# A long depthwise convolution beside a state-space scan: one of eight channel groups computed by ScalarE and GpSimd

## The chip, the cores and the metric

The kernel runs on one core of a Trainium2 chip, in one launch. The metric is the time of the device in microseconds. The kernel before takes 2796.59 us, the median of three runs (2795.34 to 2796.99).

## The reference

The reference computes, for 512 tokens of width 1024, one block of attention with its MLP (`first_block`) and then two layers of a second block (`second_block`), all in fp32. The change lies in the mixer of the second block's first layer, the "even" mixer:

```python
def even_mixer(x, w_in, conv_w, conv_b, conv_ln_g, conv_ln_b, ssm_conv_w, ...):
    proj = x @ w_in
    conv_val, conv_gate, z, xbc, dt = jnp.split(proj, [c0, c1, c2, c3], axis=-1)
    u = conv_val * jax.nn.sigmoid(conv_gate)
    u = causal_depthwise_conv(u, conv_w, conv_b)        # 31 taps, 1024 channels
    u = jax.nn.silu(layer_norm(u, conv_ln_g, conv_ln_b))
    xbc = jax.nn.silu(causal_depthwise_conv(xbc, ssm_conv_w, ssm_conv_b))   # 4 taps
    ...
    y = ssd_chunked(xs * dt, dt * a, bm, cm)            # scan over 4 chunks of 128 tokens
    y = (y + xs * d_skip) * jax.nn.silu(z)
    y = rms_norm(y by group of 512)
    return jnp.concatenate([u, y], axis=-1) @ w_out
```

The layer goes on with a cross attention over 256 memory tokens and an MLP. The products that make the memory's keys and values do not depend on the mixer.

## The kernel before, in words

**Products.** Channels lie on the 128 partitions, tokens in the free dimension. Every fp32 product is made of three products of rounded fp32 ("fp32r"): high activation by high weight, low activation by high weight, high activation by low weight (L923, L925, L927). A *unit* is one group of 128 output channels for 512 tokens: 24 matmuls of 128x128 by 128x512. For each of the eight tiles of the depth the three follow each other in that order, so the third matmul of a unit is the first that reads the low weight. ScalarE rounds each weight tile (L1539, `round_ahead` L1528), VectorE (L2323) or GpSimd (L3412, `lower_ahead`) subtracts the rounded tile from the original and so makes the low part. Three tiles of high weights and five raw tiles are held; each engine rounds or lowers up to two units ahead, at the place where its own program calls `run_steps` or `round_ahead`. In the gate and value part of the even mixer GpSimd makes the low parts. DMA queues of SyncE load the weights.

**Order.** No scheduler runs on the chip: each engine has its own instruction list, written out by a Python function for it, and the engines meet at semaphores. A wait in a list holds everything that stands behind it on that engine. The lists follow one plan (`plans`, from L296). For the even mixer it is:
- "ev lead" and "ev gv": 8 gate units (`evg`) and 8 value units (`evv`), three of them in the lead, and between them `dt`. Counted from 0, the 14 steps of "ev gv" are evv1, dt, evg2, evg3, evv2, evv3, evg4, evg5, evv4, evv5, evg6, evg7, evv6, evv7. VectorE makes the product of value and sigmoid after each value unit (L2494).
- "ev xbc": 10 units in the order 0, 1, 2, 3, 8, 10, 4, 5, 6, 7, then "ev xbc end": 9 and 11. Each is copied from PSUM by ScalarE (L1526), convolved with 4 taps by VectorE (L2508), and made into silu by `xbc_half` (ScalarE, L1721, with L1725 and L1729) and `xbc_end` (VectorE, L2456), which come one unit later, behind the next unit's short convolution.
- 16 scan steps (4 chunks by 4 quarters of the heads). For each, ScalarE makes `E1` (L2012) and four exponentials, VectorE the masked decay (`scan_mask` L2968, `scan_decay` L2980), GpSimd two products (L3551, L3562), TensorE the products. Every second step carries one `z` unit. Before them, at step 6 of "ev gv", ScalarE makes the exponential `dte` (L1999), for which VectorE has computed the exponent (`step_widths` L2903, L2954, L2957).
- The gated rms norm (squares by L3036, sums by TensorE at L1008), the first half of the output product (`yout`), with the memory's value and key units (`mv`, `mk`; 256 tokens) between its units.
- "conv wait": three memory units. Then the sums of the convolution's layer norm over all channels (L1350 to L1356), the eight `("conv norm", k)` parts with one or two memory units each, and the rest of the output product.

**The long convolution.** The 1024 channels are 8 groups of 128. ScalarE makes tap 0 of a group into a PSUM bank (`conv_first` L1954) and VectorE adds taps 1 to 30 there, one instruction each, `bank = input shifted by t times tap weight + bank` (`long_tap` L2443, L2450). Two banks hold two groups at a time: even groups in bank 3, odd ones in bank 7 (`conv_bank`, L707). The taps of two groups are interleaved, since each tap reads the sum that the last one of its group wrote; an interleaved tap takes some 0.66 us, one that directly follows another of its group some 0.79. After tap 30 ScalarE copies the group out with its bias and makes its square (`conv_out` L1964, L1968, L1974), GpSimd adds both to the running sums (`conv_inputs` L3528), and `conv_first(m + 2)` takes the bank again.

All 240 taps of VectorE have slots (L736 to L753): 6 in the lead, 8 behind each of the 14 steps of "ev gv", 3 behind each of the first 8 xbc units, 3 in each scan step, 2 to 5 in the items of "y out", and the rest, 7, in "conv wait". The ends of the groups follow from it:

| group | 0 | 1 | 2 | 3 | 4 | 5 | 6 | 7 |
|---|---|---|---|---|---|---|---|---|
| ends in slot | gv 5 | gv 6 | gv 13 | xbc unit 0 | scan 10 | scan 12 | y out 13 | conv wait |

`conv_out(slot)` stands in ScalarE's list behind the unit of that slot, and so ahead of the rounding of the weights for the next unit that has not been rounded yet.

**Places for the rest.** `zT` holds the gated z, 8 groups; it is not written before the scan. `sq_rings["conv"]` holds the squares on their way to GpSimd.

The slots of the taps in the kernel before, lines 740 to 744:

```python
        tap_slots = {("gv", "lead"): 6} | {("gv", i): 8 for i in range(14)} | {("xbc", m): 3 for m in XBC_ORDER[:8]}
        tap_slots |= {("scan", st): 3 for st in STEPS}
        out_items = plans["y lead"] + plans["y out"]
        tap_slots |= {("y out", i): 0 if isinstance(u, Step) else 3 if u.name != "yout" else 2 if i < 3 else 5
                      for i, u in enumerate(out_items)}
```

## Time and profile before

| | |
|---|---|
| median of three runs | 2796.59 us (2795.34 to 2796.99) |
| the profiled execution | 2796.68 us, of which the span of the instructions is 2794.9 |
| TensorE's mean granted clock | 0.972 |
| TensorE matmul busy | 2659.7 us, 95% |
| VectorE busy | 1477.1 us, 53% |
| ScalarE busy | 1123.1 us, 40% |
| GpSimd busy | 406.5 us, 15% |
| the 240 taps of VectorE (L2450) | 167.9 us |
| the 91 low parts of GpSimd (L3412) | 195.5 us |

The profile is of one execution. All times in rows are from the start of its span. The profiled execution took 1.8 us more than its span: what lies before the first and behind the last instruction. Engines are named PE (TensorE's matmuls), PEld (its weight loads, which lie beside matmuls), DVE (VectorE), ACT (ScalarE) and POOL (GpSimd). The granted clock is a share of full speed: 1.0 is 2.4 GHz and a half is 1.2 GHz. The part of the even mixer that the change touches runs from about 1000 us to about 1435 us: gate and value part to 1110, xbc to 1190, scan to 1272, its end and the gated norm to 1301, the first half of the output product with the memory's units to 1361, the convolution's norm to 1435.

In a row of a timeline the brackets say for how long the engine had stood idle before the instruction, and which instruction's end let it go on.

### The profile page before, as it was taken

The page shows a single profiled execution, that of the slowest core. Times are in us where ns is not written, and L with a number is a line of the kernel's source. Part 1 is how long each engine was busy: PE and PEld are TensorE (multiplying, and loading weights), DVE is VectorE, ACT ScalarE, POOL GpSimd, SP SyncE. Part 2 cuts the span into 40 slices and gives each one's busy share as a digit, 9 for nine tenths or more (in the row PEclk, how much of TensorE's full clock was granted, in tenths as well). Part 3 has the DMA queues.
Part 4 walks back from the last instruction along what each step waited for, and adds up shares of the span by engine and source line. Part 5 has one row for each costly group of instructions (what it writes and reads, how often), then busy time and mean ns, then how long its engine had stood idle before and what let it go on. Part 6 is the DMA issues. An engine that isn't in the chain of part 4 may idle for free.

```text
span 2794.9 us, 33638 instructions
## 1 busy us (share of the span) xinstructions
PE 2659.7 (95%) x13661; PEld 2192.6 (78%) x13661; DVE 1477.1 (53%) x2551; ACT 1123.1 (40%) x1845; POOL 406.5 (15%) x295
## 2 busy tenths in 40 slices
PE   6998799999999999998999999999999999999998
PEld 6775567778888987786886778889788886888887
DVE  3366866345333279798874643333734743642334
ACT  2455344235332243645554443322642543542323
POOL 0032123110000024443110111000000100110000
PEclk6999899999999999999999999999999999999999
DMA  8343223442333333212431233333221341233331
GB/s 222 98 109 82 76 69 94 118 112 83 98 92 97 91 85 85 81 38 68 129 90 53 68 91 91 98 92 90 76 83 38 102 125 45 84 91 98 92 97 61
DMA packets 483306, 251.31 MB, mean 90 GB/s; under 512 B 15582, under 2 KB 480050, under 8 KB 483151
## 3 DMA queue, kind: packets, MB, share of 16 engines
q1 hardware_dynamic: 480596, 242.56, 30.8%
q0 software_dynamic: 1840, 5.59, 0.6%
q8 instruction: 107, 1.75, 0.3%
q10 hardware_dynamic: 715, 1.01, 0.1%
q14 instruction: 48, 0.39, 0.0%
HBM read 247.00 MB, written 2.13 MB: 89 GB/s over the span
## 4 chain that ended last, share of the span: by engine, by line
PE 79%; DVE 13%; ACT 6%; issue 1%; POOL 0%; DMA 0%; SPq 0%; POOLq 0%; DVEq 0%; ACTq 0%
PE ps L927 19%; PE ps L923 19%; PE ps L925 19%; PE ps L859 2%; PE ps L855 2%; PE ps L857 2%; PE ps L949 2%; DVE ps L2450 2%; PE ps L883 1%; DVE w_r L2323 1%; PE ps L1395 1%; PE ps L1078 1%; PE ps L873 1%; PE ps L875 1%; PE ps L1093 1%
## 5 line engine op out<-in xcount | busy, mean ns | idle before, releaser
L923 PE MATMUL ps<-XH,wh 128*128 128x512 f32 (+2 forms) x1896 | 769.2, 406 | 11.0 <-ACT arena_f L1729 3.7
L927 PE MATMUL ps<-XH,w_r 128*128 128x512 f32 (+2 forms) x1896 | 753.6, 397 | 5.8 <-DVE w_r L2323 4.0
L925 PE MATMUL ps<-XL,wh 128*128 128x512 f32 x1776 | 709.0, 399 | 3.0 <-DVE XL L2834 2.8
L2323 DVE TENSOR_TENSOR w_r<-w_f,wh 128x1024 fp32r<-128x1024 f32 (+1 forms) x316 | 378.7, 1200 | 566.5 <-ACT wh L1539 566.4
L1539 ACT ACTIVATE wh<-w_f 128x1024 fp32r<-128x1024 f32 (+2 forms) x407 | 411.0, 1012 | 390.6 <-PE ps L927 209.9
L923 PEld LDWEIGHTS ps<-XH,wh 128*128 128x128 f32 (+2 forms) x1896 | 359.3, 190 | 120.1 <-issue 19.7
L927 PEld LDWEIGHTS ps<-XH,w_r 128*128 128x128 f32 (+2 forms) x1896 | 357.6, 189 | 94.3 <-DVE w_r L2323 6.6
L925 PEld LDWEIGHTS ps<-XL,wh 128*128 128x128 f32 x1776 | 335.5, 189 | 86.0 <-issue 4.4
L925 PE MATMUL ps<-arena_r,wh 128*128 128x512 f32 (+1 forms) x936 | 343.1, 367 | 0.0
L923 PE MATMUL ps<-arena_r,wh 128*128 128x512 f32 (+1 forms) x726 | 265.1, 365 | 1.4 <-ACT wh L1539 1.4
L927 PE MATMUL ps<-arena_r,w_r 128*128 128x512 f32 (+1 forms) x726 | 259.9, 358 | 6.2 <-DVE w_r L2323 6.2
L3412 POOL TENSOR_TENSOR w_r<-w_f,wh 128x1024 fp32r<-128x1024 f32 (+4 forms) x91 | 195.5, 2150 | 421.2 <-ACT wh L1539 421.1
L925 PEld LDWEIGHTS ps<-arena_r,wh 128*128 128x128 f32 x936 | 178.1, 190 | 30.7 <-issue 1.9
L857 PE MATMUL ps<-arena_r,wh 128*128 128x256 f32 x672 | 188.9, 281 | 0.0
L2450 DVE SCALAR_TENSOR_TENSOR ps<-arena_f,vec,ps 128x512 f32<-128x512 f32 x240 | 167.9, 750 | 6.9 <-ACT ps L1526 5.9
L1688 ACT ACTIVATE arena_f<-ps 128x512 f32<-128x512 f32 x96 | 57.1, 595 | 266.6 <-PE ps L927 252.5
L927 PEld LDWEIGHTS ps<-arena_r,w_r 128*128 128x128 f32 x726 | 138.6, 191 | 28.2 <-DVE w_r L2323 7.2
L923 PEld LDWEIGHTS ps<-arena_r,wh 128*128 128x128 f32 x726 | 138.7, 191 | 27.7 <-issue 5.4
L1526 ACT ACTIVATE arena_f<-ps 128x512 f32<-128x512 f32 (+6 forms) x198 | 89.5, 468 | 171.1 <-PE ps L927 120.5
L3459 POOL TENSOR_TENSOR arena_f<-arena_f 128x512 f32<-128x512 f32 x48 | 55.0, 1145 | 536.8 <-ACT arena_f L1688 536.8
L857 PEld LDWEIGHTS ps<-arena_r,wh 128*128 128x128 f32 x672 | 126.9, 189 | 0.4
L855 PE MATMUL ps<-arena_r,wh 128*128 128x256 f32 x420 | 118.6, 282 | 0.0
(383 smaller groups left out, 3816.2 us busy)
## 6 DMA issues: line engine op xcount, KB each, us to landing
w_f<-in_mlp_w SPq DMA_DIRECT2D x126, 512.0 KB, 4.1
w_f<-in_w_ff SPq DMA_DIRECT2D x63, 512.0 KB, 4.0
w_f<-in_w_in SPq DMA_DIRECT2D x49, 512.0 KB, 3.8
w_f<-in_ada_w SPq DMA_DIRECT2D x35, 512.0 KB, 4.0
w_f<-in_even_w_in SPq DMA_DIRECT2D x35, 512.0 KB, 3.8
w_f<-in_odd_w_in SPq DMA_DIRECT2D x23, 512.0 KB, 3.8
w_f<-in_even_w_out SPq DMA_DIRECT2D x16, 512.0 KB, 4.1
w_f<-in_xa_w_v SPq DMA_DIRECT2D x16, 512.0 KB, 4.1
```

What stands on the lines that cost most here:

```text
L855: e.matmul(b, hi[:, k, :], xh[:, hs], start=u.first and k == 0, stop=False)
L857: e.matmul(b, hi[:, k, :], xl[:, hs], start=False, stop=False)
L859: last = e.matmul(b, lo[:, k, :], xh[:, hs], start=False, stop=u.final and k == u.kc - 1)
L923: e.matmul(b, hi[:, k, :], xh, start=u.first and k == 0, stop=False)
L925: e.matmul(b, hi[:, k, :], xl, start=False, stop=False)
L927: last = e.matmul(b, lo[:, k, :], xh, start=False, stop=u.final and k == u.kc - 1)
L1526: return e.activation(o, i, ACT.Copy, scale=scale).then_inc(act.sem, act.up(*mark))
L1539: e.activation(high_flat(u), flat(u, 0), ACT.Copy).then_inc(act.sem, act.up("high", u.n))
L1688: e.activation(ffn_h[:, m, :], b, ACT.Relu).then_inc(act.sem, act.up("ff relu", st, m))
L2323: e.tensor_tensor(flat(u, 1), flat(u, 0), high_flat(u).bitcast(F32), ALU.subtract).then_inc(dve.sem, dve.up("low", u.n))
L2450: e.scalar_tensor_tensor(out=o, in0=val[:, m, t:t + S], scalar=conv_tap(t, m), in1=o, op0=ALU.mult, op1=ALU.add).then_inc(dve.sem, dve.up( ...
L3412: e.tensor_tensor(flat(u, 1), flat(u, 0), high_flat(u).bitcast(F32), ALU.subtract).then_inc(pool.sem, pool.up("low", u.n))
```

## The change

- **One group off VectorE.** `POOL_GROUP = 2`. Its sum stands in `zT[:, 7]` in SBUF. ScalarE makes tap 0 there, and each further tap as a scaled copy into one of four tiles (`scaled(t)` is `zT[:, 3 + t % 4]`); GpSimd adds it to the sum. Three taps stand behind each of the steps 5 to 13 of "ev gv" and one behind each of the first three xbc units, after the engine's `run_steps` of that step. ScalarE's copy of tap t waits for GpSimd's add of tap t - 4, and each add for the one before. The group is copied out and squared behind the eighth xbc unit (5 is its channel group).
- **210 taps on VectorE in other slots**: 6 in the lead, 7 behind each step of "ev gv", 3 behind each of the ten xbc units of "ev xbc", 6 in a new slot "xbc end" between the short convolutions of units 9 and 11, 2 in each scan step, 1, 2 or 4 in the items of "y out", and 7 in "conv wait". Groups 0, 3, 5, 7 and 1, 4, 6 follow each other in the two banks. The groups end as follows:

| group | 0 | 1 | 2 | 3 | 4 | 5 | 6 | 7 |
|---|---|---|---|---|---|---|---|---|
| ends in slot | gv 6 | gv 7 | xbc unit 5 | xbc unit 2 | xbc unit 10 | y out 0 | y out 6 | conv wait |

- **Weights rounded first.** Where a group ends, ScalarE calls `round_ahead` for the next unit before it waits for the group's last tap (`conv_out(..., before=...)`).
- **The end of xbc.** The silu parts of the last three units (7, 9, 11) no longer stand behind the next unit's short convolution: `xbc_half(7)` stands behind ScalarE's first exponential of the scan, and `xbc_end(7)` behind VectorE's `scan_mask(0)`; those of 9 and 11 stand directly behind their own units.
- **The sums of the convolution's norm** come in TensorE's list behind one memory unit, not three. The norm's parts 0 and 1 have two memory units each, not 2 and 1, so that no unit is added or dropped.
- GpSimd adds the groups to the running sums in the order in which they end (`conv_input`). No product and no tap is left out.

The diff, cut to its core:

```diff
-    plans["conv wait"] = [next(kv) for _ in range(3)]
+    plans["conv wait"] = [next(kv) for _ in range(2)]
     for k in range(KC):
-        plans["conv norm", k] = [next(kv) for _ in range(1 if k else 2)]
+        plans["conv norm", k] = [next(kv) for _ in range(2 if k < 2 else 1)]
...
-        conv_bank = [banks[3], banks[7]]
+
+        conv_at = [banks[3 if j % 2 == 0 else 7] for j in range(KC)]
+        conv_at[POOL_GROUP:] = [zT[:, KC - 1, :]] + conv_at[POOL_GROUP:-1]
+
+        def scaled(t):
+
+            return zT[:, 3 + t % 4, :]
...
-        tap_slots |= {("scan", st): 3 for st in STEPS}
+
+        groups = [m for m in range(KC) if m != POOL_GROUP]
+        taps = [(groups[0], t) for t in range(1, CONV_W)]
+        for j in range(1, len(groups)):
+            ahead = 6 if j % 2 else 28
+            at = (j - 1) * (CONV_W - 1) + ahead
+            taps[at:] = [v for t in range(1, CONV_W)
+                         for v in ([(groups[j - 1], t + ahead)] if t + ahead < CONV_W else []) + [(groups[j], t)]]
+        tap_slots = {("gv", "lead"): 6} | {("gv", i): 7 for i in range(14)} | {("xbc", m): 3 for m in XBC_ORDER[:XBC_FIRST]}
+        tap_slots |= {("xbc end",): 6}
+        tap_slots |= {("scan", st): 2 for st in STEPS}
         out_items = plans["y lead"] + plans["y out"]
-        tap_slots |= {("y out", i): 0 if isinstance(u, Step) else 3 if u.name != "yout" else 2 if i < 3 else 5
+        tap_slots |= {("y out", i): 0 if isinstance(u, Step) else 2 if i == 4 or u.name != "yout" else 1 if i < 3 else 4
                       for i, u in enumerate(out_items)}
-        tap_slots["conv wait",] = (CONV_W - 1) * KC - sum(tap_slots.values())
...
+        pool_taps = {("gv", i): 3 for i in range(5, 14)} | {("xbc", m): 1 for m in XBC_ORDER[:3]}
...
-            run("conv wait")
+            run_units(plans["conv wait"][:1])
...
             sq_rings["conv"].free(pe, "conv", KC - 1)
+            run_units(plans["conv wait"][1:])
             for k in range(KC):
...
-                    if m:
+                    if 0 < XBC_ORDER.index(m) < XBC_FIRST:
                         xbc_half(XBC_ORDER[XBC_ORDER.index(m) - 1])
...
+                if m in groups[:2]:
+                    w.wait_ge(*(lin, att4)[groups.index(m)].held("conv"))
+                elif m != POOL_GROUP:
+                    w.wait_ge(act, "sq", "conv", groups[groups.index(m) - 2])
...
+            def own_taps(*slot):
+
+                for t in [next(tap_of) for _ in range(pool_taps.get(slot, 0))]:
+                    if t > 4:
+                        w.wait_ge(pool, "conv", POOL_GROUP, t - 4)
+                    copy(scaled(t), val[:, POOL_GROUP, t:t + S], "tap", t, scale=conv_tap(t, POOL_GROUP))
...
+                e.activation(conv[:, m, :], conv_at[m][:, :], ACT.Identity, bias=column("even_conv_b_2", m)).then_inc(
...
+                if m in groups[:-2]:
+                    conv_first(groups[groups.index(m) + 2])
+
+            def conv_out(*slot, before=None):
...
                 for m in conv_ends[slot]:
-                    w.wait_ge(dve, "conv", m)
...
-                    if m + 2 < KC:
-                        conv_first(m + 2)
+                    if before:
+                        round_ahead(before.n)
+                    conv_end(m, dve)
...
 
             conv_first(0)
+            nexts = dict(zip(plans["ev gv"] + plans["ev xbc"], plans["ev gv"][1:] + plans["ev xbc"] + plans["ev xbc end"]))
             for i, u in enumerate(plans["ev gv"]):
                 run_steps([u])
-                if i == 0:
-                    conv_first(1)
+                if u.name == "evv" and u.m in (groups[1], POOL_GROUP):
+                    conv_first(u.m)
                 if i == 3:
                     flush()
                     log1p_exp_minus(dt_, sc1, sc2, sc3, "dt")
                 if i == 6:
                     w.wait_ge(dve, "dte")
                     e.activation(dte, dte, ACT.Exp).then_inc(act.sem, act.up("dte"))
-                conv_out("gv", i)
+                own_taps("gv", i)
+                conv_out("gv", i, before=nexts[u])
...
                 e.activation(E1, bb, ACT.Exp).then_inc(act.sem, act.up("e1", st))
+                if st == 0:
+                    xbc_half(XBC_ORDER[XBC_FIRST - 1])
...
             for u in plans["ev xbc"]:
                 run_steps([u])
-                if ("xbc", u.m) in conv_ends:
-                    conv_out("xbc", u.m)
+                own_taps("xbc", u.m)
+                conv_out("xbc", u.m, before=nexts[u])
+                if u.m == XBC_ORDER[7]:
+                    conv_end(POOL_GROUP, pool)
             scan_groups(0, 0)
             scan_decay(0)
-            run("ev xbc end")
-            xbc_half(XBC_ORDER[-1])
+
+            zs = {st: plans["scan", st | 1][0] for st in STEPS}
+            for u in plans["ev xbc end"]:
+                run_steps([u])
+                xbc_half(u.m)
+                if u.m == XBC_ORDER[XBC_FIRST]:
+                    conv_out("xbc end", before=plans["ev xbc end"][1])
...
-                conv_out("scan", st)
+                conv_out("scan", st, before=zs.get(st))
...
-                    conv_out("y out", n)
-            run_steps(plans["conv wait"][:2])
-            conv_out("conv wait")
-            run_steps(plans["conv wait"][2:])
+                    conv_out("y out", n, before=plans["conv wait"][0] if i == len(out_items) - 1 else None)
+            conv_out("conv wait", before=plans["conv wait"][0])
+            run("conv wait")
...
             scan_mask(0)
+            xbc_end(XBC_ORDER[XBC_FIRST - 1])
             scan_decay(0)
-            run("ev xbc end")
+            run_steps(plans["ev xbc end"][:1])
+            conv_taps("xbc end")
+            xbc_end(XBC_ORDER[XBC_FIRST])
+            run_steps(plans["ev xbc end"][1:])
             xbc_end(XBC_ORDER[-1])
...
+            def own_taps(*slot):
+
+                o, m = conv_at[POOL_GROUP], POOL_GROUP
+                for t in [next(tap_of) for _ in range(pool_taps.get(slot, 0))]:
+                    w.wait_ge(act, "tap", t)
+                    if t > 1:
+                        w.wait_ge(pool, "conv", m, t - 1)
+                    e.tensor_tensor(o, o, scaled(t), ALU.add).then_inc(pool.sem, pool.up("conv", m, t))
+                    if t == CONV_W - 1:
+                        pool.marks["conv", m] = pool.count
...
+                own_taps("xbc", u.m)
+                conv_inputs("xbc", u.m)
+                if u.m == XBC_ORDER[7]:
+                    conv_input(POOL_GROUP)
...
-            run("ev xbc end")
+            run_steps(plans["ev xbc end"][:1])
+            conv_inputs("xbc end")
+            run_steps(plans["ev xbc end"][1:])
```

## Rows read from the trace of the kernel before

**Rows 1.** The page: engine busy time, and the chain that ended last
```profile
PE 2659.7 (95%) x13661; PEld 2192.6 (78%) x13661; DVE 1477.1 (53%) x2551; ACT 1123.1 (40%) x1845; POOL 406.5 (15%) x295
...
PE 79%; DVE 13%; ACT 6%; issue 1%; POOL 0%; DMA 0%; SPq 0%; POOLq 0%; DVEq 0%; ACTq 0%
```

**Rows 2.** Busy time by stretch: PE, PEld, DVE, ACT, POOL, granted clock, DMA share, GB/s
```profile
1015.00:1110.00 95.00, 90.38 (x394) 70.47 (x393) 88.55 (x137) 30.16 (x42) 37.79 (x19) 0.96 0.32 89
...
1190.00:1272.00 82.00, 81.84 (x514) 71.21 (x512) 75.47 (x138) 38.54 (x95) 40.39 (x31) 0.98 0.14 39
...
1272.00:1301.00 29.00, 19.50 (x78) 14.23 (x79) 27.33 (x42) 20.34 (x30) 6.70 (x4) 0.82 0.22 73
```

**Rows 3.** Timeline, TensorE alone: start us, us, what [idle before <-releaser]
```profile
1069.09 0.79 PE L927 MATMUL ps<-XH,w_r 128*128 128x512 f32 x1 [1.71 <-POOL w_r L3412]
...
1082.26 0.39 PE L923 MATMUL ps<-XH,wh 128*128 128x512 f32 x1
...
1116.15 0.40 PE L927 MATMUL ps<-XH,w_r 128*128 128x512 f32 x1
...
1171.65 0.50 PE L923 MATMUL ps<-XH,wh 128*128 128x512 f32 x1 [2.78 <-ACT arena_f L1729]
...
1281.61 0.46 PE L1253 MATMUL ps<-arena_f 128*128 128x128 f32 x2 [4.20 <-DVE arena_f L2980]
...
1296.19 2.08 PE L1008 MATMUL ps<-stat,ones 128*128 128x512 f32 x2 [2.17 <-DVE stat L3036]
...
1366.11 0.58 PE L927 MATMUL ps<-arena_r,w_r 128*128 128x256 f32 x1 [3.33 <-DVE w_r L2323]
...
1405.83 0.50 PE L927 MATMUL ps<-XH,w_r 128*128 128x512 f32 x1 [1.10 <-DVE w_r L2323]
```

**Rows 4.** Timeline, ScalarE alone
```profile
1063.57 0.69 ACT L1968 ACTIVATE arena_f<-ps,vec 128x512 f32<-128x512 f32 x1 [16.01 <-DVE ps L2450]
...
1065.50 1.04 ACT L1539 ACTIVATE wh<-w_f 128x1024 fp32r<-128x1024 f32 x1
...
1070.29 0.26 ACT L1999 ACTIVATE arena_f<-arena_f 128x64 f32<-128x64 f32 x1 [1.84 <-DVE arena_f L2957]
...
1267.24 0.69 ACT L1968 ACTIVATE arena_f<-ps,vec 128x512 f32<-128x512 f32 x1 [2.28 <-DVE ps L2450]
...
1377.26 1.28 ACT L1651 ACT_TABLE_LOAD   x1
```

**Rows 5.** Timeline, VectorE alone
```profile
1019.50 4.71 DVE L2450 SCALAR_TENSOR_TENSOR ps<-arena_f,vec,ps 128x512 f32<-128x512 f32 x6 [0.76 <-ACT ps L1526]
...
1052.38 0.68 DVE L2494 SCALAR_TENSOR_TENSOR arena_f<-gates,ps 128x512 f32<-128x512 f32 x1
...
1123.51 1.23 DVE L2456 SCALAR_TENSOR_TENSOR arena_f<-arena_f 128x512 f32<-128x512 f32 x1
...
1178.84 2.34 DVE L2508 SCALAR_TENSOR_TENSOR ps<-arena_f,vec,ps 128x512 f32<-128x512 f32 x3 [5.45 <-ACT ps L1526]
...
1269.78 0.69 DVE L2968 TENSOR_TENSOR arena_f<-ps,const 128x512 f32<-128x512 f32 x1 [2.58 <-ACT arena_f L2012]
...
1357.46 7.48 DVE L2450 SCALAR_TENSOR_TENSOR ps<-arena_f,vec,ps 128x512 f32<-128x512 f32 x10
...
1379.22 0.75 DVE L3133 SCALAR_TENSOR_TENSOR arena_f<-arena_f,vec,stat 128x512 f32<-128x512 f32 x1 [0.94 <-ACT stat L1651]
```

**Rows 6.** GpSimd: timeline, and one tile's instructions (duration ns min/median/max)
```profile
1073.55 7.12 POOL L3412 TENSOR_TENSOR w_r<-w_f,wh 128x1024 fp32r<-128x1024 f32 x3
...
L3459 POOL TENSOR_TENSOR arena_f<-arena_f x48: 1040/1041/1671, 660.3 to 2592.9; 128x512 f32<-128x512 f32 x48
...
L3551 POOL TENSOR_TENSOR arena_f<-arena_f x16: 1262/1276/1369, 1163.9 to 1278.2; 128x512 f32<-128x512 f32 x16
...
2072.57 0.63 POOL L3626 TENSOR_SCALAR_AFFINE_SELECT arena_f<-arena_f 128x512 f32<-128x512 f32 x1 [107.78 <-ACT arena_f L1526]
...
2073.28 0.42 POOL L3629 TENSOR_SCALAR_AFFINE_SELECT arena_f<-arena_f 128x256 f32<-128x256 f32 x1
```

More of the change, by code:

```diff
@@ L73 @@
 XBC_FIRST = 10
+POOL_GROUP = 2
 def t5_bucket(n):
@@ L731, in program @@
         split_to = splits_of()
-        taps = [(0, t) for t in range(1, CONV_W)]
-        for m in range(1, KC):
-            ahead = 6 if m % 2 else 28
-            at = (m - 1) * (CONV_W - 1) + ahead
-            taps[at:] = [v for t in range(1, CONV_W) for v in ([(m - 1, t + ahead)] if t + ahead < CONV_W else []) + [(m, t)]]
-        tap_slots = {("gv", "lead"): 6} | {("gv", i): 8 for i in range(14)} | {("xbc", m): 3 for m in XBC_ORDER[:8]}
-        tap_slots |= {("scan", st): 3 for st in STEPS}
+        groups = [m for m in range(KC) if m != POOL_GROUP]
[8 more added lines that the diff above has]
+        tap_slots |= {("scan", st): 2 for st in STEPS}
         out_items = plans["y lead"] + plans["y out"]
-        tap_slots |= {("y out", i): 0 if isinstance(u, Step) else 3 if u.name != "yout" else 2 if i < 3 else 5
+        tap_slots |= {("y out", i): 0 if isinstance(u, Step) else 2 if i == 4 or u.name != "yout" else 1 if i < 3 else 4
                       for i, u in enumerate(out_items)}
-        tap_slots["conv wait",] = (CONV_W - 1) * KC - sum(tap_slots.values())
+        tap_slots["conv wait",] = (CONV_W - 1) * len(groups) - sum(tap_slots.values())
         slot_taps, conv_ends, taps_done = {}, {}, 0
@@ L752, in program @@
             taps_done += n
-        assert sorted(v for ts in slot_taps.values() for v in ts) == [(m, t) for m in range(KC) for t in range(1, CONV_W)]
+        assert sorted(v for ts in slot_taps.values() for v in ts) == [(m, t) for m in groups for t in range(1, CONV_W)]
+        pool_taps = {("gv", i): 3 for i in range(5, 14)} | {("xbc", m): 1 for m in XBC_ORDER[:3]}
+        assert sum(pool_taps.values()) == CONV_W - 1
         def chunk_of(u, k):
@@ L1954, in conv_first @@
             def conv_first(m):
-                if m < 2:
-                    w.wait_ge(*(lin, att4)[m].held("conv"))
-                else:
-                    w.wait_ge(act, "sq", "conv", m - 2)
+                if m in groups[:2]:
+                    w.wait_ge(*(lin, att4)[groups.index(m)].held("conv"))
+                elif m != POOL_GROUP:
+                    w.wait_ge(act, "sq", "conv", groups[groups.index(m) - 2])
                 w.wait_ge(dve, "val", m)
                 w.wait_ge(dve, "half taps")
-                copy(conv_bank[m % 2][:, :], val[:, m, 0:S], "first", m, scale=conv_tap(0, m))
@@ L1964, in conv_out @@
-            def conv_out(*slot):
-                for m in conv_ends[slot]:
-                    w.wait_ge(dve, "conv", m)
-                    e.activation(conv[:, m, :], conv_bank[m % 2][:, :], ACT.Identity, bias=column("even_conv_b_2", m)).then_inc(
-                        act.sem, act.up("conv out", m))
-                    s = conv_q
-                    if m:
-                        s, freed = sq_rings["conv"].take("conv", m)
-                        w.wait_ge(*freed)
-                    e.activation(s, conv_bank[m % 2][:, :], ACT.Square, bias=column("even_conv_b_2", m)).then_inc(
-                        act.sem, act.up("sq", "conv", m))
-                    if m + 2 < KC:
-                        conv_first(m + 2)
+                copy(conv_at[m][:, :], val[:, m, 0:S], "first", m, scale=conv_tap(0, m))
@@ new lines, in scalar_program, with conv_end @@
+            tap_of = iter(range(1, CONV_W))
+            def own_taps(*slot):
[3 more added lines that the diff above has]
+                    copy(scaled(t), val[:, POOL_GROUP, t:t + S], "tap", t, scale=conv_tap(t, POOL_GROUP))
+            def conv_end(m, progress):
+                w.wait_ge(progress, "conv", m)
+                e.activation(conv[:, m, :], conv_at[m][:, :], ACT.Identity, bias=column("even_conv_b_2", m)).then_inc(
+                    act.sem, act.up("conv out", m))
+                s = conv_q
+                if m:
+                    s, freed = sq_rings["conv"].take("conv", m)
+                    w.wait_ge(*freed)
+                e.activation(s, conv_at[m][:, :], ACT.Square, bias=column("even_conv_b_2", m)).then_inc(
+                    act.sem, act.up("sq", "conv", m))
+                if m in groups[:-2]:
+                    conv_first(groups[groups.index(m) + 2])
@@ L2443, in long_tap @@
             def long_tap(m, t):
-                o = conv_bank[m % 2][:, :]
+                o = conv_at[m][:, :]
                 if t == 1:
@@ L2511, in evacuate @@
                     raw_ring.free(dve, m)
-                    if m:
+                    if 0 < XBC_ORDER.index(m) < XBC_FIRST:
                         xbc_end(XBC_ORDER[XBC_ORDER.index(m) - 1])
```

28 lines of the change are left out of this document (17 added, 11 removed).

## The prediction, before the result was known

> **What bounds the kernel now.** I read the page first: TensorE is busy for 95% of the span and is most of the chain that ended last [rows 1]. Only its idle time and its half-speed time can be won. The busy time by stage comes next [rows 2]: the even mixer is where VectorE is nearly as busy as TensorE. TensorE's waits there, and the single matmuls after each wait [rows 3], give four places. (a) 1063.6 to 1069.1: idle 5.1 us in the gate and value part. (b) 1168.7 to 1171.65: 2.9 us, a bank that xbc unit 9 holds. (c) 1277 to 1296: the end of the scan, 4.4 us before the last output step and more before the products and the sums of the gated norm. (d) 1361 to 1366.1: low weights behind the last taps. In the scan proper (1190:1272) TensorE is busy for all 82 us though VectorE is too: taps taken out of there win nothing by themselves, they only let VectorE reach the scan's end less late.
>
> **The sum** is made against the profiled execution, 2796.7 us (span 2794.9), 0.1 above the median of the three runs, 2796.6. Signs: plus is slower. "Unit" is one 24-matmul product, 5.57 us.
>
> **1. Place (a): the new rounding point.** Now ScalarE waits for group 0's last tap until 1063.57, only then rounds (1065.50), GpSimd lowers, and TensorE gets its low weights at 1069.09 [rows 3, 4]. The change rounds ahead of the sums, and VectorE has 7 taps a slot, not 8. But at step 6 ScalarE has a second wait ahead of all this: dte (row L1999 at 1070.29), which VectorE makes behind slot 6's taps [rows 4, 5]. The new time of dte: evv2's product at 1052.4 - 0.66 = 1051.7 (one tap fewer in the dt chain); two times (0.6 + 7 x 0.66) = 10.4 to 1062.2; nacs and 7 taps, 4.9, to 1067.1; dte read by ScalarE at 1067.3. Behind it in ScalarE's queue stand the exponential 0.2, three scaled taps 1.8 and the rounding 1.1: to 1070.4. GpSimd must add taps 4 to 6 first (from 1068.1, 3.9) and then lower (2.4): 1074.5. The unit that stalled now runs 1063.6 to 1069.2, and the next one, at its third matmul at 1069.7, waits for that low part: 4.8 us, against 5.1. The stall moves one unit on; the half-speed stretch that follows it (mean granted clock 0.96 over these 95 us [rows 2]) moves with it. Term: **0** (that unit ended at 1082.26, it would end at 1082.2). The three ScalarE operations per step cost nothing more here: ScalarE is busy 30 of 95 us [rows 2].
>
> **2. GpSimd as the bound.** From gv step 5 GpSimd has, per unit, one lowering, 2.38 us, and three adds into one accumulator. No row shows this add. Its nearest row is L3551, 128x512 in the same arena with two different inputs: 1.28 [rows 6]. Each add waits for the one before; a waiting pair there starts 0.07 after its predecessor's end (L3626 0.63, L3629 0.71 later), an independent one 0.04 before it. So a step costs 2.38 + 1.35 + 1.35 + 1.24 = 6.3 us where TensorE needs 5.57. From tap 4 at 1068.1 up to the low part of the third xbc unit stand in GpSimd's queue: 8 lowerings 19.0, 24 adds 31.5, and the two sum adds of group 1, 2.5: 53.0, to 1121.1. That unit's third matmul ran at 1116.15 [rows 3]. Term: **+5.0**, seen as some 0.7 us of idle in each of seven units. The lower bound is L3459's 1.04 (both inputs the same tile): 5.5 a step, no bound, term 0. The upper bound is its longest, 1.67: 24 x 0.39 more, term +14.4. I take 1.28, by the row with two inputs. ScalarE's wait for a free one of four slots (tap t for add t - 4) holds nobody: three adds stand ready whenever it waits.
>
> **3. xbc and its end.** Place (b) goes: unit 9's half is made right after the first exponential. But units 6 and 7 now have three taps between their short convolution (2.0 us later), and six taps (4.0) stand between the short convolutions of units 9 and 11. Unit 11's short convolution ended at 1181.2 [rows 5]; on the old clock it would now end at 1163.8 + 2.0, xbc_end, inputs and mask 1.9, exponentials and rounding 2.3, copies 1.3, short convolution 2.3, taps 4.0, xbc_end 0.6, short convolution 2.3: 1180.5. TensorE waits for it in the first scan steps instead of at (b). Three group ends move into xbc, each 2 us of ScalarE, within a bank's slack of 3 us. Term: **-0.5** (bounds 0 and -2.9).
>
> **4. The end of the scan.** 16 taps leave it, 10.6 us of VectorE, and both group ends. ScalarE's 2.3 us wait for a tap at 1267.24, which made the mask late (1269.78) [rows 4, 5], is gone. Seg 14 comes from TensorE at 1266.2 as now; exponential, mask, exponentials and product of step 14 end at 1269.9, group inputs (4.6 beside a lowering) at 1274.9, z 1275.5, mask 15 1276.2, exponentials 1277.5, product 1278.4, where TensorE now starts at 1281.61 [rows 3]: 3.2 earlier. After that one tap less and no lag: rstd at 1285.3, first high part at 1286.8 (was 1291.4), the g1 sums at 1291.4 where they ran at 1296.19. Term: **-4.8** (bounds: 0 if another wait holds the chain; -8.0 if the half-speed stretches behind 0.82 [rows 2] go too).
>
> **5. Output part.** TensorE has no gap from 1300 to 1361, so 12 taps fewer win nothing before the last ones. Group 7's last 13 taps now stand alone, in series at 0.79 (the ten at 1357.46 took 7.48, seven of them in series [rows 5]), with one lowering: 1353.0 + 10.3 + 1.1 = 1364.4, against 1364.8. The sums no longer stand behind two value products, so TensorE idles from 1359 to 1365.1 and they end at 1367.1 at half speed, not 1374.9. But ScalarE now evacuates a value product that runs behind them before its tables and the rstd: the product ends at 1371.8, two evacuations 0.8, two table loads of 1.28 [rows 4], logarithm and exponential 1.4, so 1376.5, against 1379.2 for the first norm [rows 5]. VectorE then carries ten lowerings, not nine (+1.1), to the one that releases the output products at 1405.83 [rows 3]. Term: -2.7 + 1.1 = **-1.6** (bounds 0 and -3.4, the latter with TensorE never waiting after the sums).
>
> **Total**: 0 + 5.0 - 0.5 - 4.8 - 1.6 = -1.9. Predicted 2794.8 us. A change of 0.2%, 5.6 us, is about what a measurement of this kernel can tell from none.
>
> **Rivals.**
> **A, cheap adds.** The add costs 1.04 like L3459, the median of its 48 rows. Then term 2 is 0 and the time 2794.8 - 5.0 = 2789.8. Against it: L3551, with two different inputs, never went below 1.26 [rows 6]. The Trainium skill ("GPSIMD Engine Reference", 3.1 Elementwise) gives about 2.6 cycles an element for a two-input add; at that page's 1.2 GHz an estimate of 1.1 us for 512, which would take 4 us from term 2 and put the time at 2790.7. L3551's row is 0.17 above that figure. Chance 0.18.
> **B, the stall at (a) really goes.** If dte is ready early, GpSimd's queue of 53.0 starts at 1062.8 and ends at 1115.8, before the third xbc unit needs it at 1116.15: terms 1 and 2 together are -0.3, not +5.0, and the time 2794.8 - 5.3 = 2789.5. For it: the rounding is what the old chain waits for. Against it: dte's wait stands in the code and in the trace. Chance 0.15.
> **C, the tail gives nothing back.** Another wait takes the scan's end (the squares, the table loads of 1.28): term 4 is 0, 2799.6. Chance 0.1.
> **D, slower: adds and taps hold each other.** L3459 has rows of 1.67, and a VectorE product with both inputs in SBUF goes from 0.68 to 1.23 beside GpSimd [rows 5, 6]. If each add cost 1.67, term 2 is +14.4 and the time 2804. It decides from an add of 1.6 us. Against it: a tap has one operand in PSUM, and 6 of them took 4.71 beside a lowering, the usual 0.66 each [rows 5]. Chance 0.12.
> **The forecast case**: 0.45, its own range 2790.5 to 2798.5.
> That the change does not do what it says would be seen in the counts below; the diff leaves no room for it.
>
> **The numbers.** The range takes A, B, C and the forecast with their bounds: 2788.5 to 2801. Faster by over 0.2% (under 2791.0): most of A and B and a tail of the forecast, 0.31. Slower by over 0.2% (over 2802.2): D and a little of C, 0.13. Between: 0.56.
>
> **What would show it.** Step 1: no idle at the unit that starts at 1063.6, some 5 us at the next one, ended by GpSimd's low part, and ScalarE waiting for dte at about 1067. Step 2: GpSimd busy over 90% from 1068 to 1121, adds 1.28 long at 1.35, TensorE waiting for L3412's low part seven times. Step 3: no wait for L1729 before unit 11. Step 4: the last scan output 3 us less behind its predecessor. Step 5: 30 fewer taps on VectorE (210), TensorE idle before the conv sums. I am wrong if TensorE's waits for GpSimd come to less than 3 us or more than 9, or if a fresh wait of over 2 us stands in the scan or the output part.

## The result, and the profile after

The changed kernel takes 2802.24 us, the median of 20 runs (2799.45 to 2803.39), against 2795.66 for the kernel before (2794.39 to 2798.18) in the same 20 rounds: a ratio of 1.0022, 95% interval 1.0015 to 1.0029. It is 6.6 us slower. 2794.8 was forecast, and the range ended at 2801. The profiled execution took 2802.54, its span is 2800.8, 5.9 above the span before.

The experiments below are medians of 5 to 11 runs, in three sets of rounds: e1 to e4, with the kernel before at 2796.60 in the same rounds; e5 to e8, with it at 2796.25; e9 and e10, with it at 2796.06. The figure behind each median is the ratio to the kernel before of its own rounds, with its 95% interval. In the last set two runs at a mean clock of 0.647 and 0.554 (3727 us for e9, 4331 us for the kernel before) stand apart from all others, and the ratios leave them out.

The page of the kernel after, first its busy times, then the chain that ended last, then the group of TensorE's third matmuls (busy, mean, and how long it stood idle before them):

```profile
PE 2661.7 (95%) x13661; PEld 2190.9 (78%) x13661; DVE 1456.9 (52%) x2521; ACT 1142.8 (41%) x1875; POOL 447.7 (16%) x325
...
PE 78%; DVE 11%; ACT 6%; issue 3%; POOL 2%; DMA 0%; SPq 0%; POOLq 0%; DVEq 0%; ACTq 0%
...
L942 PE MATMUL ps<-XH,w_r 128*128 128x512 f32 (+2 forms) x1896 | 752.9, 397 | 12.9 <-POOL w_r L3457 8.9
```

Against [rows 1] VectorE has 30 instructions fewer, ScalarE and GpSimd 30 more each, and GpSimd now has 2% of the chain, where it had none. The last row holds most of the loss: TensorE waits 8.9 us for low parts that GpSimd makes (L3412 before is L3457 now; L927 is L942). With the wait of 3.62 us at 1318.96 below, which stands in another row of the page, its waits for GpSimd's low parts are ten and come to 12.5 us; before they were two and 1.9.

Busy time by stretch, columns as in [rows 2]:

```profile
1015.00:1110.00 95.00, 87.52 (x382) 67.24 (x381) 76.81 (x122) 45.01 (x65) 62.38 (x39) 0.98 0.32 89
...
1190.00:1272.00 82.00, 80.09 (x508) 70.40 (x508) 70.79 (x134) 35.55 (x91) 36.52 (x30) 0.96 0.14 39
1272.00:1301.00 29.00, 22.96 (x100) 17.59 (x100) 26.44 (x40) 21.77 (x34) 7.25 (x5) 0.82 0.24 73
1301.00:1361.00 60.00, 56.38 (x297) 47.81 (x296) 35.77 (x51) 20.86 (x31) 23.72 (x12) 0.97 0.33 96
```

VectorE fell from 88.6 to 76.8 us in the gate and value part, GpSimd rose from 37.8 to 62.4, and TensorE fell from 90.4 to 87.5: the work left VectorE, for which TensorE had waited only around place (a) of the prediction, and went to the engine for which it then waited in every unit. TensorE, eight of its waits in the order of time:

```profile
1073.41 0.50 PE L942 MATMUL ps<-XH,w_r 128*128 128x512 f32 x1 [3.54 <-POOL w_r L3457]
...
1082.13 0.50 PE L942 MATMUL ps<-XH,w_r 128*128 128x512 f32 x1 [1.34 <-POOL w_r L3457]
...
1121.03 0.50 PE L942 MATMUL ps<-XH,w_r 128*128 128x512 f32 x1 [0.65 <-POOL w_r L3457]
...
1188.27 0.30 PE L1291 MATMUL ps<-const,arena_f 128*128 128x128 f32 x1 [2.93 <-DVE arena_f L2497]
...
1282.43 0.35 PE L1268 MATMUL ps<-arena_f 128*128 128x128 f32 x1 [1.90 <-DVE arena_f L3021]
...
1318.96 0.50 PE L942 MATMUL ps<-arena_r,w_r 128*128 128x512 f32 x1 [3.62 <-POOL w_r L3457]
...
1370.62 1.22 PE L1369 MATMUL ps<-arena_f,ones 128*128 128x512 f32 x1 [4.93 <-ACT arena_f L1992]
...
1411.39 0.50 PE L942 MATMUL ps<-XH,w_r 128*128 128x512 f32 x1 [1.09 <-DVE w_r L2364]
```

The row at 1318.96 has no counterpart in [rows 3]: before, TensorE was busy from 1300 to 1361 without a gap.

TensorE's 13,661 matmuls stand in the same order in all these kernels, but for a few around the convolution's sums. So the start of the same-numbered matmul in two traces can be compared, and the difference at 1003 us, ahead of the change, taken off (it is 0.3 for the kernel after, and between -1.6 and 1.7 for the experiments). The columns are times of the kernel before, the entries microseconds later than before (negative is earlier). Each line is one execution; those of e6 and e10 are the slowest of their runs, 3.5 and 3.2 us above the median:

```
                  1119    1189    1271    1299    1328    1357    1473    2391    2791
after             4.71    4.65    3.88   -0.10    5.29    5.29    5.29    5.45    5.57
e1 sums later     4.69    4.62    3.91   -0.08   -0.05   -0.05   -0.76   -3.75   -4.11
e2 two adds      -3.53   -2.52   -3.07   -7.30   -3.29   -3.29   -2.54   -4.01   -3.81
e3 both          -3.55   -2.55   -3.07   -7.28   -7.08   -7.08   -6.10   -7.77   -7.61
e4 round only     1.76    3.29    5.11    3.75    3.41    3.41    3.42    3.51    3.45
e5 four adds     11.28   11.22   10.63    6.47    6.65    6.65    6.01    2.79    3.02
e6 dte later     -7.06   -6.06   -6.53  -10.81  -10.53  -10.53   -9.56  -11.11  -10.88
e7 tail only      0.01    0.02    0.00    0.00   -0.01   -0.01   -0.41   -0.19   -0.36
e8 tail back     -3.53   -2.51   -3.05   -7.26   -7.06   -7.06   -7.31   -7.19   -7.61
e9 no end taps   -7.05   -7.82   -9.11  -13.09  -13.35  -13.35  -19.43  -20.87  -21.17
e10 scan three   -7.05   -6.05   -3.87   -4.44   -3.93   -3.93   -6.08   -7.77   -7.62
```

The first line is the whole story of the change: 4.7 lost up to the third xbc unit, nothing in xbc, 4.75 won back in the scan (0.8 in its first steps, 4.0 at its end), and 5.4 lost between 1309 and 1328: 3.8 by the wait and 1.6 by the half speed that follows it (1320.4 to 1323.8). GpSimd there, and the same engine in the gate part:

```profile
1088.53 4.19 POOL L3603 TENSOR_TENSOR arena_f<-arena_f 128x512 f32<-128x512 f32 x3
1092.67 2.40 POOL L3457 TENSOR_TENSOR w_r<-w_f,wh 128x1024 fp32r<-128x1024 f32 x1
1095.03 4.17 POOL L3603 TENSOR_TENSOR arena_f<-arena_f 128x512 f32<-128x512 f32 x3
...
1314.31 1.08 POOL L3580 TENSOR_TENSOR stat<-stat,arena_f 128x512 f32<-128x512 f32 x1 [26.54 <-ACT arena_f L1992]
1315.36 1.26 POOL L3585 TENSOR_TENSOR arena_f<-arena_f,sq 128x512 f32<-128x512 f32 x1
1316.58 7.00 POOL L3457 TENSOR_TENSOR w_r<-w_f,wh 128x1024 fp32r<-128x1024 f32 x3
```

At 1314 GpSimd has been idle for 26.5 us. ScalarE had rounded a weight tile by about 1312.5, but GpSimd could not lower it: the two adds of group 5 into the running sums stand ahead in its list, and they wait for ScalarE's copy of the group. The low part was ready at 1318.9; before, GpSimd began it at 1312.5. The reason is a difference between two lists. `conv_out` and `conv_inputs` both follow the slots, but ScalarE calls those of the items 0, 1 and 2 of "y out" together at item 2, behind its roundings, and GpSimd calls each at its own item. The low parts of the next units come behind item 0 (in e1 below two of them stand ahead of the moved sums, and the third behind). Before, no group ended in items 0 to 2. Now group 5 ends in item 0.

### The profile page after: what moved, and what is told of

It reads as the page before. It is cut to its first block, busy times and chain, and to the rows that moved or that the text cites. A ratio compares the mean times of both kernels' runs of the same rounds, so it can differ in the third digit from the quotient of the medians.

```text
span 2800.8 us, 33696 instructions
## 1 busy us (share of the span) xinstructions
PE 2661.7 (95%) x13661; PEld 2190.9 (78%) x13661; DVE 1456.9 (52%) x2521; ACT 1142.8 (41%) x1875; POOL 447.7 (16%) x325
## 4 chain that ended last, share of the span: by engine, by line
PE 78%; DVE 11%; ACT 6%; issue 3%; POOL 2%; DMA 0%; SPq 0%; POOLq 0%; DVEq 0%; ACTq 0%
PE ps L942 19%; PE ps L938 19%; PE ps L940 19%; PE ps L874 2%; PE ps L870 2%; PE ps L872 2%; PE ps L964 2%; PE ps L898 1%; DVE ps L2491 1%; PE ps L1411 1%; PE ps L888 1%; PE ps L1093 1%; PE ps L890 1%; DVE w_r L2364 1%; POOL arena_f L3603 1%
## 5 line engine op out<-in xcount | busy, mean ns | idle before, releaser
L942 PE MATMUL ps<-XH,w_r 128*128 128x512 f32 (+2 forms) x1896 | 752.9, 397 | 12.9 <-POOL w_r L3457 8.9
L942 PEld LDWEIGHTS ps<-XH,w_r 128*128 128x128 f32 (+2 forms) x1896 | 356.7, 188 | 104.0 <-POOL w_r L3457 12.8
L942 PE MATMUL ps<-arena_r,w_r 128*128 128x512 f32 (+1 forms) x726 | 259.4, 357 | 6.1 <-POOL w_r L3457 3.6
L3457 POOL TENSOR_TENSOR w_r<-w_f,wh 128x1024 fp32r<-128x1024 f32 (+4 forms) x91 | 194.6, 2141 | 351.3 <-ACT wh L1555 351.3
L942 PEld LDWEIGHTS ps<-arena_r,w_r 128*128 128x128 f32 x726 | 137.9, 190 | 28.3 <-POOL w_r L3457 4.0
L2491 DVE SCALAR_TENSOR_TENSOR ps<-arena_f,vec,ps 128x512 f32<-128x512 f32 x210 | 148.7, 750 | 14.5 <-ACT ps L1542 12.9
```

Source lines behind the costliest of these rows:

```text
L942: last = e.matmul(b, lo[:, k, :], xh, start=False, stop=u.final and k == u.kc - 1)
L2491: e.scalar_tensor_tensor(out=o, in0=val[:, m, t:t + S], scalar=conv_tap(t, m), in1=o, op0=ALU.mult, op1=ALU.add).then_inc(dve.sem, dve.up( ...
L3457: e.tensor_tensor(flat(u, 1), flat(u, 0), high_flat(u).bitcast(F32), ALU.subtract).then_inc(pool.sem, pool.up("low", u.n))
```

## The experiments

**e1, the sums behind the low parts.** GpSimd's list is brought in line with ScalarE's.

```diff
                     lower_ahead(u.n)
-                conv_inputs("y out", i)
+                if i >= 2:
+                    for n in (0, 1, 2) if i == 2 else (i,):
+                        conv_inputs("y out", n)
```

> Edit of the changed kernel: GpSimd adds group 5 to the running sums behind its three low parts of item 2 of "y out", not ahead of them. Theory Q (GpSimd's queue): TensorE's idle time of 3.8 us at 1315 and the slow clock behind it go, the time falls by 5 us from 2802.2 to about 2797. Rival V (the wait moves): the low part is late for another reason, or the late sums delay the convolution's sums; then the stall stays within 1 us or comes back before 1375, and the time is 2801 to 2803.

Measured: 2793.17 us, 0.9991 of before (0.9982 to 1.0000). By the table the stall is gone, 5.3 us between 1299 and 1328. GpSimd's timeline in e1:

```profile
1313.25 4.77 POOL L3457 TENSOR_TENSOR w_r<-w_f,wh 128x1024 fp32r<-128x1024 f32 x2 [24.94 <-ACT wh L1555]
1317.99 1.08 POOL L3580 TENSOR_TENSOR stat<-stat,arena_f 128x512 f32<-128x512 f32 x1
```

Theory Q holds for the place and the size. The median fell by 9.1, not 5: the other 3 to 4 us stand behind 1473, in a part that no edit touches (below, on the clock). Against the kernel before the interval reaches 1.0000: e1 is hardly to be told from it.

**e2, two adds a step.**

```diff
-        pool_taps = {("gv", i): 3 for i in range(5, 14)} | {("xbc", m): 1 for m in XBC_ORDER[:3]}
+        pool_taps = {("gv", i): 2 for i in range(5, 14)} | {("xbc", m): 2 if j < 4 else 1 for j, m in enumerate(XBC_ORDER[:8])}
```

> Edit of the changed kernel: the same 30 taps of group 2, two (not three) behind each step 5 to 13 of "ev gv", the other 12 over the first eight xbc units. Theory Q: GpSimd needs 2.38 + 2 x 1.38 = 5.1 us a step, under TensorE's 5.57; the seven gaps of 0.8 us from 1080 to 1121 go, the time falls by 5 to 2797. Rival S (adds and taps share something: each add slows VectorE or TensorE's operands wherever it stands): the number of adds is the same, so the loss stays, 2801 to 2803, and VectorE's or TensorE's instructions are longer than before in the xbc units.

Measured: 2792.60, 0.9984 (0.9975 to 0.9992). The column 1119 falls from 4.71 to -3.53, by 8.2 where 5 were expected: the repeated gaps are gone, and the first stall is shorter too (idle 2.14 instead of 3.54, since two adds and not three stand ahead of that low part, and no half-speed stretch at 1075). The number of adds is the same, so rival S falls. Group 5's stall is still there, 3.61 us at 1311.54; no half speed follows it here, and it costs 3.8 us (columns 1299 and 1328), where it cost 5.4 in the kernel after.

**e3, both.** e1's and e2's edits together.

> Both edits of the changed kernel together (sums behind the low parts, two adds a step). Theory Q: both losses go, 10 us, to about 2792, 3.5 us under the kernel before (2795.7), which is what the scan's end and the convolution's norm give back. Rival V: time won in the gate part is lost again at the next wait for VectorE or ScalarE; 2796 or more.

Measured: 2786.98, 0.9964 (0.9950 to 0.9978). Both losses are gone (columns 1119 and 1328), and up to 1357 nothing takes their place. The time fell by 5 us more than expected. By the trace 2.4 of these are there by 1357, of which 1.0 is lost again by 1473; 1.8 stand behind 1473, and 1.6 ahead of 1003.

**e5, four adds a step**, in e1's kernel.

```diff
-        pool_taps = {("gv", i): 3 for i in range(5, 14)} | {("xbc", m): 1 for m in XBC_ORDER[:3]}
+        pool_taps = {("gv", i): 4 if i < 12 else 2 for i in range(5, 13)}
```

> Edit of the changed kernel with group 5's sums behind the low parts (e1): the 30 taps four behind each step 5 to 11 of "ev gv" and two behind step 12. Theory Q (GpSimd's work per step is the bound): 2.38 + 4 x 1.38 = 7.9 us a step against 5.57, 2.3 us lost in each of seven steps, 16 in all, against 5.4 with three: 10 us above e1's 2793, about 2803. Rival N (only the number of adds counts, or the last add's time): the total work of GpSimd is the same, so within 2 us of e1.

Measured: 2800.02, 1.0014 (1.0005 to 1.0023), 6.9 above e1 where Q said 10 and N at most 2. In the column 1119 it is 6.6 above e1. GpSimd:

```profile
1092.82 5.60 POOL L3603 TENSOR_TENSOR arena_f<-arena_f 128x512 f32<-128x512 f32 x4
1098.37 2.36 POOL L3457 TENSOR_TENSOR w_r<-w_f,wh 128x1024 fp32r<-128x1024 f32 x1
1100.67 5.57 POOL L3603 TENSOR_TENSOR arena_f<-arena_f 128x512 f32<-128x512 f32 x4
```

A step takes 7.85 us, as worked out. What was wrong is how long it lasts. The sixth low part, counted from the stall's own at 1072.48, starts at 1114.13 (1105.63 in the kernel after) with six adds more in front of it: 8.5 us later. Then two adds are left, while with three a step two more steps lose 6.50 - 5.57 = 0.93 us each: 6.6 in all. The rate per step decides, not the total: rival N falls.

**e4, the rounding ahead alone**, in the kernel before. All taps and groups stay.

```diff
                 for m in conv_ends[slot]:
+                    if before:
+                        round_ahead(before.n)
                     w.wait_ge(dve, "conv", m)
...
-                conv_out("gv", i)
+                conv_out("gv", i, before=nexts[u])
```

(and so for xbc, scan and the last item of "y out")

> Edit of the kernel before: only the rounding of the next weights ahead of a group's sums; all taps on VectorE in their old slots. Theory Q (dte's wait takes over): the idle time at 1063 to 1069 moves by one unit at most and keeps its size, the time is within 1 us of before. Rival R (rounding is what it waited for): the 5 us of idle and half-speed time go, 2791.

Measured: 2799.40, 1.0011 (1.0003 to 1.0020), 2.8 slower. Rival R falls: the stall does not go. It moves to the next unit and grows by 1.8 (table, 1119). ScalarE's and TensorE's timelines of e4:

```profile
1069.13 0.26 ACT L2003 ACTIVATE arena_f<-arena_f 128x64 f32<-128x64 f32 x1 [2.81 <-DVE arena_f L2961]
1069.30 1.04 ACT L1539 ACTIVATE wh<-w_f 128x1024 fp32r<-128x1024 f32 x1
```

```profile
1070.48 0.47 PE L923 MATMUL ps<-XH,wh 128*128 128x512 f32 x1 [2.32 <-ACT wh L1539]
1075.66 0.80 PE L927 MATMUL ps<-XH,w_r 128*128 128x512 f32 x1 [4.48 <-POOL w_r L3416]
```

ScalarE waits for dte and only then rounds. A second cost is new. By 1189 e4 loses 1.5 more (half-speed time at 1172 that the kernel before does not have), and from 1189 to 1271 another 1.8. VectorE's decay product there:

```profile
1259.90 2.81 DVE L2984 TENSOR_TENSOR arena_f<-arena_f 128x512 f32<-128x512 f32 x1
```

and GpSimd beside it:

```profile
1258.52 1.30 POOL L3555 TENSOR_TENSOR arena_f<-arena_f 128x512 f32<-128x512 f32 x1
1259.77 2.39 POOL L3416 TENSOR_TENSOR w_r<-w_f,wh 128x1024 fp32r<-128x1024 f32 x1
```

The same product (L2980 of the kernel before) took 0.69 at 1264.67 and 1256.76. Rounded earlier, the weights are lowered earlier, and the low part now falls on a product that TensorE waits for. This last 1.8 comes back at the scan's end (1299: 3.75, 1328: 3.41); what remains of e4's loss is the 1.8 of the stall and the 1.5 at 1172.

**e6, dte two steps later**, in e3's kernel.

```diff
-                if i == 6:
+                if i == 8:
                     w.wait_ge(dve, "dte")
```

> Edit of e3: ScalarE takes its exponential dte, and its wait for it, behind step 8 of "ev gv", not 6. Theory D (that wait holds ScalarE's scaled taps, GpSimd's adds and the low part behind them): TensorE's idle 2.3 us at 1068 and 1.7 us at 1076 go, and the time falls by 4 from e3's 2787 to 2783. Rival R: group 0's last tap, which ScalarE waits for in the same step, holds the chain instead; within 1 us of e3.

Measured: 2783.13, 0.9953 (0.9941 to 0.9966), 3.9 under e3, and 3.5 in the column 1119. TensorE has no wait over 0.6 us from 1040 to 1155. Theory D holds: the last wait of ScalarE in that step is the one for dte, as the prediction's step 1 said.

**e7, the convolution's sums earlier, alone**, in the kernel before.

```diff
-            run("conv wait")
+            run_units(plans["conv wait"][:1])
...
+            run_units(plans["conv wait"][1:])
             for k in range(KC):
```

(with the counts of the memory units of the change, and ScalarE's order)

> Edit of the kernel before: only the convolution's sums one memory unit earlier in TensorE's list (two in "conv wait", two in the norm's part 1), the rounding ahead of the last group. Step 5 as measured by the change's trace: 0.7 to 1.6 us faster than before. Rival E (the early sums only make TensorE stand idle for the last taps): 0 to 3 us slower.

Measured: 2795.07 against 2796.25, 0.9994 (0.9985 to 1.0003): no difference that the runs can tell. In the trace it is 0.4 faster (column 1473 against 1357), and all of it is there by 1406.

**e8, the sums back where they were**, in e3's kernel: the reverse of e7's edit.

> Edit of e3: the convolution's sums back behind three memory units, as in the kernel before, everything else as in e3. Step 5: 0.7 to 1.6 us slower than e3's 2787. Rival E: 0 to 3 us faster than e3, since the 5.3 us in which TensorE stands idle before the sums are filled by the two units.

Measured: 2789.82, 0.9975 (0.9966 to 0.9985), 2.8 above e3. But the traces of e8 and e3 end at the same distance (-7.61 both), and differ by 3.0 us ahead of 1003 us, where the two have the same instructions: 2.3 of it stand by 75 us, at the start of the program. So the 2.8 are not the sums' doing, as far as the profile shows. At 1387, behind the sums, e3 is 7.45 and e8 7.28 ahead of before, at 1406 7.69 and 7.28. Then the clock parts them: e3 waits 1.09 us at 1396.81 and runs at half speed from 1397.3 to 1400.7, e8 waits 1.08 at 1400.25 and does not, and in the column 1473 e8 is ahead by 1.2. Whether the sums' place has a part in that is not shown. The expectation's size was not met, and what makes the first microseconds differ between kernels stays open.

**e9, no taps between units 9 and 11**, in e6's kernel.

```diff
-        tap_slots |= {("xbc end",): 6}
+        tap_slots |= {("xbc end",): 0}
...
-        tap_slots |= {("y out", i): 0 if isinstance(u, Step) else 2 if i == 4 or u.name != "yout" else 1 if i < 3 else 4
+        tap_slots |= {("y out", i): 0 if isinstance(u, Step) else 3 if u.name != "yout" or i < 2 else 2 if i == 2 else 5 if i < 9 else 4
```

> Edit of e6: none of the six taps between the short convolutions of units 9 and 11; six more in the items of "y out" instead. Theory X (the six taps, 4.0 us of VectorE in front of unit 11's short convolution, are what TensorE waits for when the scan starts): its idle 4.2 us at 1174 goes, and with it a part of the half-speed time behind it; 4 to 7 us under e6's 2783, 2776 to 2779. Rival R: unit 11's own product, copy and silu hold the first scan step; within 1.5 us of e6.

Measured: 2774.57, 0.9921 (0.9905 to 0.9937): 8.6 under e6 and 21.5 under before, the fastest version. (The four runs of the usual clock have 2774.3 as their median; the traces of e6 and e9 are 10.3 apart at the end.) TensorE in e9:

```profile
1175.47 0.30 PE L1291 MATMUL ps<-const,arena_f 128*128 128x128 f32 x1 [2.22 <-DVE arena_f L2497]
...
1347.69 1.13 PE L1369 MATMUL ps<-arena_f,ones 128*128 128x512 f32 x2 [0.97 <-ACT arena_f L1992]
```

The wait at the scan's start fell from 4.00 us (e6, at 1178.13) to 2.22, with part of the half-speed time behind it: 2.6 us by column 1271, less than the 4 to 7 of theory X. The larger part was not in the expectation, and goes, as far as this one edit shows, with a second difference in it. The edit put 12 taps more than before into "y out", six from "xbc end" and six out of "conv wait", where one is left. So TensorE's wait before the convolution's sums is 0.97 us, not 4.93, and no clock fall follows: column 1357 to 1473 is -6.1 here and 0.0 in the kernel after. "y out" had room: VectorE is busy there for 35.8 of 60 us in the kernel after.

**e10, three taps in each scan step**, in e6's kernel.

```diff
-        tap_slots |= {("scan", st): 2 for st in STEPS}
+        tap_slots |= {("scan", st): 3 for st in STEPS}
```

(with 17 taps fewer in "y out" and one more in "conv wait")

> Edit of e6: three taps in each scan step, not two, as in the kernel before (groups 5 and 6 end in scan steps 10 and 13), 16 taps fewer in "y out". Step 4 (the taps taken out of the scan are what brings its end forward): TensorE's output of the last scan step and the two waits behind it come 4 to 5 us later, 2787 to 2788. Rival C (the tail of the scan gives nothing back): within 1 us of e6's 2783.

Measured: 2786.91, 0.9967 (0.9955 to 0.9978), 3.8 above e6. Rival C falls. At the scan's end (1299) it is 6.4 behind e6; 3 of it come back at the convolution's sums, for which TensorE waits 3.35 us, not 4.93, with no half speed behind. TensorE, before the output of the last scan step:

```profile
1278.41 0.77 PE L1268 MATMUL ps<-arena_f 128*128 128x128 f32 x2 [4.90 <-DVE arena_f L3021]
```

## Why the prediction was wrong

The sum was -1.9 and the traces give +5.57. Step by step:

**Steps 1 and 2**, 0 and +5.0: measured together +4.71. The closeness of the sum is partly luck. The stall moved to the next unit and stayed, but smaller (idle 3.54 at 1073.41 where 4.8 was worked out, half speed from 1074.6 to 1078.0): the unit that was to end at 1082.2 as before ended at 1080.2. GpSimd's queue then took that back and more. It began at 1066.90, not 1068.1, and needed 54.1 us, not 53.0, so that its end came out right: the third matmul of the third xbc unit ran at 1121.03, against 1121.1 worked out. That dte's wait causes the stall, e4 and e6 confirm; in ScalarE's timeline of the kernel after it stands ahead of the scaled taps:

```profile
1065.95 0.26 ACT L2031 ACTIVATE arena_f<-arena_f 128x64 f32<-128x64 f32 x1 [7.06 <-DVE arena_f L2998]
1066.11 1.94 ACT L1542 ACTIVATE arena_f<-arena_f,vec 128x512 f32<-128x512 f32 x3
1067.95 1.04 ACT L1555 ACTIVATE wh<-w_f 128x1024 fp32r<-128x1024 f32 x1
```

An add takes 1.295 us (1.261 to 1.309 over 30), against the 1.28 taken from L3551; dependent adds start 1.44 apart, 0.14 behind the last one's end and not 0.07, and a step takes 6.50 (1088.53 to 1095.03) against 6.3. The waits came once with 1.34 and six times with some 0.65; each step costs TensorE 0.93, 6.50 less 5.57. Rival A's 1.04 and rival D's 1.67 are both excluded, and so is the 1.1 that rival A estimated from the Trainium skill ("GPSIMD Engine Reference", 3.1 Elementwise): the measurement decides. Rival B, the stall really gone, needs e6's edit; no run has it with three adds a step.

**Step 3**, -0.5: measured -0.06. Unit 9's wait (2.78) is gone and one of 2.93 stands before the scan's first outputs, as said.

**Step 4**, -4.8: measured -4.75 from 1189 to 1299, of which 0.8 stand in the scan's first steps and 4.0 behind 1271, where the step looked. The last output step started at 1282.43, which less the lag of 4.15 there is 1278.3, against the 1278.4 worked out. e10, which puts the 16 taps back, confirms the cause and makes it larger, 6.4.

**Step 5**, -1.6: measured 0.0. The first norm came at 1382.28, which less the 5.56 lag is 1376.7 against the 1376.5 worked out. But from there to the release of the output products VectorE needed 29.1 us and not 26.6 [rows 3, 5]. VectorE's timeline of the kernel after:

```profile
1382.28 0.75 DVE L3178 SCALAR_TENSOR_TENSOR arena_f<-arena_f,vec,stat 128x512 f32<-128x512 f32 x1 [4.46 <-ACT stat L1667]
...
1392.69 0.69 DVE L3190 SCALAR_TENSOR_TENSOR arena_f<-arena_f 128x512 f32<-128x512 f32 x1 [1.10 <-ACT arena_f L2141]
```

The step counted one low part more, 1.1; another 1.1 is the wait for ScalarE in the second row, and ScalarE had stood for 1.5 us at the copy of a memory unit (until 1390.47). By 1406 e7 against before and e3 against e8 agree: the new place of the sums is worth 0.4 us. e9, with six taps less in "conv wait", gains 6.1 over this stretch.

**What was left out**, +5.39, is the step that failed: GpSimd's list at the new end of group 5, which the sum put at nothing. It is the error that turned the sign. It is in steps 4 and 5. Step 4 counted it as a gain that "both group ends" leave the scan. Step 5 said that TensorE has no gap from 1300 to 1361, so fewer taps win nothing there, and asked nothing further of that stretch. The end of group 5 had moved into it, and with it two adds and a wait in GpSimd's list, ahead of the low parts. A group's end has a wait on ScalarE and one on GpSimd; what stands behind it was looked at for ScalarE alone. No case in the range had a loss there, so the range ended 1.2 us short of the median. With this term and the rest as it was, the sum would have been 2800.2. The signs of being wrong that the prediction named came: waits for GpSimd of 12.5 us in all, over its 9, and a fresh wait of over 2 us in the output part, at 1318.96.

The remaining 0.3 us stand behind 1473, the sum of larger pieces that go both ways (-1.6 up to 1500 us, +1.7 from 2314 to 2391). That they nearly cancel is luck.

## What to carry to other kernels

A slot table that several engines follow moves more than the work it names. When the end of something moves, follow it into each engine's list and ask what stands behind its wait; an engine that was idle for 26 us can be late by four. An engine that is given work must be compared with the bound per step, since what TensorE lost here in the gate part was still lost through xbc (4.71 at 1119, 4.65 at 1189): two adds of some 1.38 us beside a low part of 2.4 fit into 5.57 us, three do not, and the total is the same. And the last wait of a stage tells which work is worth moving: in this kernel the taps to move were the ones in "xbc end" and "conv wait" (e9 moved both at once; by the table they are worth some 2.6 and 7 us).

## What the runs showed of the hardware

**The clock falls behind a wait in one kernel and not behind the same wait in another.** Behind 1473 us all kernels have the same instructions, yet the same waits are followed by half speed in one and not in another: TensorE waits 1.44 and 0.83 us at 2257.12 and 2258.45 in the kernel after, 1.43 and 0.83 at 2253.40 and 2254.73 in e1. The granted clock of three stretches of the kernel after:

```profile
2256.00:2264.00 8.00, 6.04 (x36) 5.84 (x37) 3.66 (x3) 4.63 (x8) 0.00 (x0) 0.79 0.25 74
2346.00:2352.00 6.00, 5.03 (x9) 2.23 (x10) 1.48 (x5) 1.44 (x4) 0.00 (x0) 0.72 0.03 9
2360.00:2366.00 6.00, 5.72 (x11) 2.61 (x12) 0.69 (x1) 1.11 (x3) 0.00 (x0) 0.72 0.00 0
```

and of the same work in e1:

```profile
2250.00:2260.00 10.00, 7.74 (x64) 7.34 (x63) 4.60 (x4) 7.12 (x11) 0.00 (x0) 1.00 0.47 136
2338.00:2344.00 6.00, 4.21 (x17) 2.44 (x17) 2.10 (x8) 2.35 (x8) 0.00 (x0) 1.00 0.31 90
2355.00:2360.00 5.00, 5.00 (x19) 3.33 (x18) 2.61 (x3) 2.14 (x3) 0.00 (x0) 1.00 0.00 0
```

From 2314 to 2391 the kernel after loses 1.7 us on before, e1 wins 1.7. Runs of one kernel differ in the same way: of e1's eleven runs the three with a mean clock of 0.971 took 2797.0 to 2797.5, and the seven at 0.973 or 0.974 took 2790.5 to 2793.4. So, as an estimate from these runs, a difference of under 5 us between two versions of this kernel can be the clock's alone, and the table by stage is the better witness.

**A product of VectorE with both inputs in SBUF was held beside GpSimd.** One of 0.69 us took 2.81 beside a low part of GpSimd (e4), and ended 0.55 us behind it. Rival D weighed this for the taps, which have one operand in PSUM, and it did not reach them: their mean is 750 ns in the kernel before and in the kernel after. In e4 it reached one decay product of the 16, which had not been looked at.
